# Modulation vectors of the feed-forward stages by products on VectorE

## The reference, cut to what matters

```
mod_l = split(silu(c)     @ w_mod[i] + b_mod[i], 6)      # w_mod[i]: 1024 x 6144
mod_c = split(silu(c_ctx) @ w_mod[i] + b_mod[i], 6)
x = x + mod_l[5] * (square(relu(h @ w1)) @ w2)           # w1: 1024 x 4096, w2: 4096 x 1024
```

## Time and profile before

| | us |
|---|---|
| median of 3 runs (lowest, highest) | 3954.27 (3950.56, 3956.72) |
| profiled execution, its own time | 3956.91 |
| profiled execution, span of its instructions | 3955.1 |
| TensorE busy | 3725.2 (94% of the span) |
| VectorE busy | 1968.0 (50%) |
| ScalarE busy | 1353.3 (34%) |
| GpSimd busy | 808.4 (20%) |
| `modulation_rows` in the feed-forward stages, TensorE busy | 66.3 |

### The profile page before, as it was taken

One profiled execution on the slowest core, in us unless ns is written; L12 is line 12 of the kernel. 1 busy time (PEld: TensorE's weight loads), 2 busy tenths in 40 slices (PEclk: granted clock), 3 DMA queues, 4 the chain that ended last, 5 costly groups with the idle time before them and its releaser, 6 DMA issues. The chain is left out here.

```text
span 3955.1 us, 54396 instructions
## 1 busy us (share of the span) xinstructions
PE 3725.2 (94%) x20587; PEld 2998.3 (76%) x20587; DVE 1968.0 (50%) x2905; ACT 1353.3 (34%) x2357; POOL 808.4 (20%) x604
## 2 busy tenths in 40 slices
PE   6998899999999899999999999999999988889998
PEld 4875688888878677777776688888878865577886
DVE  5746643333353474444446653333356637746445
ACT  3346532122243454232335522121224324433222
POOL 1500012212122111222220012212110018701222
PEclk9999999999999999999999999999999998999999
DMA  5234223223211311444310023323211230032222
GB/s 179 64 117 129 65 77 121 101 89 123 95 65 64 86 44 58 175 151 149 115 60 1 1 77 129 107 85 127 95 64 54 74 132 14 19 101 92 95 95 74
DMA packets 191737, 352.38 MB, mean 89 GB/s; under 512 B 41980, under 2 KB 43597, under 8 KB 191565
## 3 DMA queue, kind: packets, MB, share of 16 engines
q1 hardware_dynamic: 183789, 333.48, 25.6%
q10 hardware_dynamic: 7792, 16.78, 1.1%
HBM read 341.71 MB, written 16.92 MB: 91 GB/s over the span
## 5 line engine op out<-in xcount | busy, mean ns | idle before, releaser
L568 POOL TENSOR_TENSOR x<-x,scaled_buf 128x512 f32<-128x512 f32 (+1 forms) x360 | 465.8, 1299 | 2274.7 <-DVE scaled_buf L560 2274.1
L129 DVE TENSOR_TENSOR w_lo<-raw,w_hi 128x2048 fp32r<-128x2048 f32 x198 | 459.1, 2319 | 796.9 <-ACT w_hi L123 785.9
L123 ACT ACTIVATE w_hi<-raw 128x2048 fp32r<-128x2048 f32 x197 | 377.2, 1915 | 1190.5 <-PE psum L385 1188.0
L383 PE MATMUL psum<-hT_hi,w_hi 128*128 128x512 f32 (+1 forms) x1888 | 668.7, 354 | 2.8 <-DVE hT_lo L787 1.5
L384 PE MATMUL psum<-hT_lo,w_hi 128*128 128x512 f32 (+1 forms) x1888 | 664.9, 352 | 0.0
L385 PE MATMUL psum<-hT_hi,w_lo 128*128 128x512 f32 (+1 forms) x1888 | 664.6, 352 | 0.0
L383 PE MATMUL psum<-w_hi,uT_hi 128*128 128x512 f32 x1280 | 503.3, 393 | 0.0
L385 PE MATMUL psum<-w_hi,uT_lo 128*128 128x512 f32 x1280 | 498.6, 390 | 0.0
L384 PE MATMUL psum<-w_lo,uT_hi 128*128 128x512 f32 x1280 | 498.2, 389 | 0.0
L560 DVE TENSOR_TENSOR scaled_buf<-psum,gate 128x512 f32<-128x512 f32 x360 | 245.2, 689 | 504.3 <-PE psum L385 499.1
L383 PE MATMUL psum<-w_hi,hT_hi 128*128 128x512 f32 x1072 | 419.9, 392 | 2.2 <-issue 1.2
(11 more groups left out here) (276 smaller groups left out, 4755.2 us busy)
## 6 DMA issues: line engine op xcount, KB each, us to landing
mod_wide<-in_w_mod SPq DMA_DIRECT2D x24, 3072.0 KB, 10.5
raw<-in_w_mlp SPq DMA_DIRECT2D x64, 1024.0 KB, 5.2
raw<-in_ff_w SPq DMA_DIRECT2D x64, 1024.0 KB, 5.3
raw<-in_ssm_w_in SPq DMA_DIRECT2D x20, 1024.0 KB, 5.1
mod_slab<-in_w_mod SPq DMA_DIRECT2D x8, 2048.0 KB, 8.1
raw<-in_b_w_qkv SPq DMA_DIRECT2D x12, 1024.0 KB, 5.1
raw<-in_a_w_qkv SPq DMA_DIRECT2D x11, 1024.0 KB, 5.0
mod_first<-in_w_mod ACTq DMA_DIRECT2D x4, 2048.0 KB, 17.2
```

The source lines that it names most:

```text
L123: act.activation(K.w_hi[h][:, :, :], K.raw[h][:, :, :], ACT.Copy).then_inc(K.hi_done.h, 1)
L129: dve.tensor_tensor(K.w_lo[h][:, :, :], K.raw[h][:, :, :], K.w_hi[h][:, :, :].bitcast(F32), ALU.subtract).then_inc(K.lo_done.h, 1)
L383: pe.matmul(out, hi_a, hi_w, start=first, stop=False, **check)
L568: pool.tensor_tensor(x, x, K.scaled_buf[:, j % 2, :], ALU.add).then_inc(K.added.h, 1)
```

## The change

VectorE now makes the products. For each of the 8 blocks `k` of 128 rows and each class, it multiplies the 768 columns of `mod_wide` with one number per partition, and adds that to an accumulator in SBUF (`mod_acc`, one for each class, [128, 2, 768]): 2 operations without and 14 with a sum, 16 in all. The first 4 of a chunk stand ahead of everything else in VectorE's body, one stands after `parts` of each latent tile, and two after each of the first four gatings of `down(0, .)`. TensorE turns each accumulator with six transposes: class 0 after `down(1, 0)`, class 1 after `down(1, 2)`, both into the same two banks. VectorE sums each over the 128 partitions that now lie along a row (`modulation_sums`). TensorE's `modulation_rows` and ScalarE's copy are gone. The load comes in two halves of 1.5 MB, the first behind the loads of the up slab, the second behind those of the down slab, each once the products that read that half before are done.

```diff
     if s.count > 2:
         if stage.chunked:
             if load_mod:
-                load_mod(sp, 0)
+                for half in range(2):
+                    load_mod(sp, 0, half, again=False)
             with sp.Fori(1, s.count // 2) as c:
                 for part in range(2):
                     for h in range(2):
                         load_half(K, sp, g0 + 2 * c + part, h, s.chunk_half(c, part, h))
-                    if load_mod and part == 0:
-                        load_mod(sp, c)
+                    if load_mod:
+                        load_mod(sp, c, part)
         elif stage.unrolled:
             for n in range(2, s.count):
                 for h in range(2):
...
     mm0, re0, sq0, uh0, ul0, sc0 = (s.n for s in (K.mm_done, K.relu_done, K.sq_done, K.u_hi_done, K.u_lo_done, K.scaled))
     FB = FF_CHUNK // P
     chunks = D_FF // FF_CHUNK
-    mu0, mo0, mt0, ma0, ml0 = K.mod_used.n, K.row_out.n, K.mod_turned.n, K.mod_added.n, K.mod_loaded[0].n
+    mt0, ms0, mp0, ml0 = K.mod_turned.n, K.mod_summed.n, K.mod_product.n, [K.mod_loaded[half].n for half in range(2)]
     MOD_W = 6 * D // chunks
     if norm is not None:
         norm.added = sc0 + 2 * nt * (chunks - 1) + nt
     mod_psum = K.psum[:, 6:8, :].rearrange("p a b -> p (a b)")[:, 0:MOD_W]
-    def load_mod(sp, c):
-
-        sp.wait_ge(K.mod_used.h, mu0 + c)
-        sp.dma_start(K.mod_wide[:, :, :], mod.w[:, :, ds(c * MOD_W, MOD_W)]).then_inc(K.mod_loaded[0].h, 16)
+    def load_mod(sp, c, half, again=True):
+        if again:
+            sp.wait_ge(K.mod_product.h, 2 * KD * c + (mp0 + KD * (half - 1)))
+        k0 = half * SLAB_K
+        sp.dma_start(K.mod_wide[:, k0:k0 + SLAB_K, :], mod.w[:, k0:k0 + SLAB_K, ds(c * MOD_W, MOD_W)]).then_inc(K.mod_loaded[half].h, 16)
+    def modulation_products(dve, c, first, last):
+        for i in range(first, last):
+            k, cls = i // 2, i % 2
+            if i % KD == 0:
+                dve.wait_ge(K.mod_loaded[i // KD].h, 16 * c + (ml0[i // KD] + 16))
+            if i == 0:
+                dve.wait_ge(K.mod_turned.h, 2 * c + mt0)
+            acc, col = K.mod_acc[:, cls, :], K.cT[:, mod.layer // 2, k, cls:cls + 1]
+            if k == 0:
+                ins = dve.tensor_scalar(acc, K.mod_wide[:, k, :], col, None, ALU.mult)
+            else:
+                dve.wait_ge(K.mod_product.h, 2 * KD * c + (mp0 + i - 1))
+                ins = dve.scalar_tensor_tensor(acc, K.mod_wide[:, k, :], col, acc, ALU.mult, ALU.add)
+            ins.then_inc(K.mod_product.h, 1)
+    def modulation_sums(dve, c, cls):
+        dve.wait_ge(K.mod_turned.h, 2 * c + (mt0 + cls + 1))
+        dve.tensor_reduce(K.mod_sum[:, 0:MOD_W // P, cls:cls + 1].rearrange("p b x -> p (b x)"), mod_psum.rearrange("p (b j) -> p b j", j=P),
+                          AX.X, ALU.add).then_inc(K.mod_summed.h, 1)
     def tile_done(eng, c, which, j):
...
                     act.activation(K.relu[:, j % 2, :], K.bank[j][:, :], ACT.Relu).then_inc(K.relu_done.h, 1)
                     square(c, j)
                 split_hi(K, act, g + 1, 1)
-                if mod:
-                    act.wait_ge(K.mod_used.h, mu0 + c + 1)
-                    act.activation(K.mod_row_wide[:, :], mod_psum, ACT.Copy).then_inc(K.row_out.h, 1)
                 if ahead:
                     split_hi(K, act, g + 2, 0)
                     if not last:
...
             def body(c, ahead, last=False):
                 g = st.g0 + 2 * c
+                if mod:
+                    modulation_products(dve, c, 0, 4)
                 split_lo(K, dve, g + 1, 0)
                 for j in range(nt):
                     parts(c, j)
+                    if mod and j < FB:
+                        modulation_products(dve, c, 4 + j, 5 + j)
                 split_lo(K, dve, g + 1, 1)
                 for h in range(2):
                     for j, t in enumerate(tiles):
...
                         gate_out(K, dve, sc0 + 2 * nt * c + h * nt + j, h, t, K.bank[j], j)
                         if norm is not None and last and h == 1:
                             norm.beside(K, dve, j)
+                        if mod and h == 0 and j < FB:
+                            modulation_products(dve, c, KD + 2 * j, KD + 2 * j + 2)
+                        if mod and h == 1 and j in (0, 2):
+                            modulation_sums(dve, c, j // 2)
                     if ahead and not (last and h):
                         split_lo(K, dve, g + 2, h)
-                if mod:
-                    dve.wait_ge(K.mod_turned.h, mt0 + c + 1)
-                    mod_sums(K, dve, mod_psum, MOD_W // P).then_inc(K.mod_summed.h, 1)
-                    dve.wait_ge(K.mod_summed.h, K.mod_summed.n + c + 1)
-                    mod_add(K, dve, mod.layer, c * (MOD_W // P), MOD_W // P).then_inc(K.mod_added.h, 1)
+                    if mod and h == 1:
+                        dve.wait_ge(K.mod_summed.h, 2 * c + (ms0 + 2))
+                        mod_add(K, dve, mod.layer, c * (MOD_W // P), MOD_W // P).then_inc(K.mod_added.h, 1)
             dve.wait_ge(K.gate_done.h, K.gate_done.n)
+            if mod:
+                dve.wait_ge(K.feat_lo.h, K.feat_lo.n)
             ahead_loop(dve, st, body, hold)
         @block.gpsimd
...
                 return product(pe, K.bank[j][:, :], K.uT_hi[:, k, t * P:(t + 1) * P], K.uT_lo[:, k, t * P:(t + 1) * P],
                                K.w_hi[h][:, k, :], K.w_lo[h][:, k, :], k == 0, k == SLAB_K - 1)
-            def modulation_rows(c):
-                pe.wait_ge(K.mod_loaded[0].h, 16 * c + (ml0 + 16))
-                pe.wait_ge(K.mod_added.h, ma0 + c)
-                mod_rows(K, pe, mod_psum[:, 0:SLAB_N], mod.layer, K.mod_wide[:, :, 0:SLAB_N])
-                mod_rows(K, pe, mod_psum[:, SLAB_N:MOD_W], mod.layer, K.mod_wide[:, :, SLAB_N:MOD_W]).then_inc(K.mod_used.h, 1)
-
-            def modulation_columns(c):
-                pe.wait_ge(K.row_out.h, mo0 + c + 1)
-                mod_turns(K, pe, mod_psum, K.mod_row_wide[:, :], MOD_W // P).then_inc(K.mod_turned.h, 1)
+            def modulation_columns(c, cls):
+                pe.wait_ge(K.mod_product.h, 2 * KD * c + (mp0 + 2 * KD - 1 + cls))
+                pe.wait_ge(K.mod_summed.h, 2 * c + (ms0 + cls))
+                mod_turns(K, pe, mod_psum, K.mod_acc[:, cls, :], MOD_W // P).then_inc(K.mod_turned.h, 1)
             def chunk(c, fed):
                 g = st.g0 + 2 * c
...
                         for k in range(SLAB_K):
                             mm = down(0, j, t, k)
                     mm.then_inc((K.w_used if j == nt - 1 else K.mm_done).h, 1)
-                    if mod and j == 2:
-                        modulation_rows(c)
                 pe.wait_ge(K.lo_done.h, 2 * g + 2)
                 for j, t in enumerate(tiles):
                     pe.wait_ge(K.scaled.h, sc0 + 2 * nt * c + j + 1)
                     for k in range(SLAB_K):
                         mm = down(1, j, t, k)
                     mm.then_inc((K.w_used if j == nt - 1 else K.mm_done).h, 1)
-                    if mod and j == 2:
-                        modulation_columns(c)
+                    if mod and j in (0, 2):
+                        modulation_columns(c, j // 2)
             chunk(0, feed is not None)
             with pe.Fori(1, chunks) as c:
...
         c = Cursor(gate_at, R + R_BYTES)
         K.gate = c.put("gate", [P, 2, D])
         K.mod_wide = c.put("mod_wide", [P, KD, 6 * P])
-        K.mod_row_wide = c.put("mod_row_wide", [P, 6 * P])
+        K.mod_acc = c.put("mod_acc", [P, 2, 6 * P])
         K.lam_in = place("lam_in", [P, 4, HEAD_DIM], H + 16 * 1024)
         K.qkv = place("qkv", [P, TOK_TILES, 3 * D], R)
         c = Cursor(qkv_end, R + R_BYTES)
```

More of the change, by code:

```diff
@@ L758, in mlp_stage @@
     if mod:
-        for s in (K.mod_used, K.row_out, K.mod_turned, K.mod_summed, K.mod_added):
-            s.n += chunks
-        K.mod_loaded[0].n += 16 * chunks
+        K.mod_added.n += chunks
+        K.mod_product.n += 2 * KD * chunks
+        for s in (K.mod_turned, K.mod_summed):
+            s.n += 2 * chunks
+        for s in K.mod_loaded[0:2]:
+            s.n += 16 * chunks
 def operand_stage(K, src, k_tiles, ctx, dst_hi, dst_lo, scale=None, bias=None, norm=None, affine=None, feat=None, gate=None, gate_scale=1.0,
@@ L2922, in program @@
         K.mod_used = sem("mod_used")
+        K.mod_product = sem("mod_product")
         K.row_out = sem("row_out")
```

## The result

| | before | after |
|---|---|---|
| median (lowest, highest), 11 runs each | 3954.46 us (3950.56, 3959.33) | 3963.06 us (3958.88, 3965.67) |
| profiled execution: own time, span | 3956.91, 3955.1 | 3962.2, 3960.3 |

The ratio is 1.0021, 95% interval 1.0013 to 1.0029: slower by 8.6 us, by 5 to 11 with the interval. The forecast was 3966, slower by 12.

A forecast was written before the change was run, and what follows sets the result against it. TensorE, busy for every microsecond of the feed-forward stages, was taken as the bound; -26 (six-tile chunks), +18 (four-tile chunks), +4 (first four-tile chunk) and +16 (clock) make +12, so 3966 us on the median, range 3930 to 3993.

The forecast's parts named there:

- The lock: VectorE operations with two SBUF inputs and GpSimd's adds wait for each other whole; a tile costs VectorE 3.54 us.
- Rival C: Products do not wait for adds, so the pace is TensorE's 2.72 us a tile; 3918 us, chance 0.13.
- The order at each gating: After each gating of down(0, .) the first product starts at g + 0.61, ahead of GpSimd's add at g + 0.76.
- rival D: The add comes first at each gating; four-tile stall 6.3 us, six-tile chunks stall 1.05; 3993 us, chance 0.12.
- Six-tile chunk: Six-tile stages: second turn stalls about 0.2 us, a chunk gains 1.95; with the exceptions, sum -26 us.
- Four-tile chunk: Four-tile stage: first turn waits 4.4 us for product 15, a chunk loses 2.25; 8 chunks +18 us.
- The first four-tile chunk: Opening of the four-tile stage: half a load arrives late, products and split start late; +4.2 us once, bounds 0 and 8.
- The clock: After each four-tile stall TensorE runs at 1.2 GHz for a while; 2 us each, bounds 0 and 2.25, +16 us.
- Rival B: The clock holds through the four-tile stage's stalls; -4 us, 3950 us, chance 0.15.
- Where nothing waits: TensorE's modulation work falls from 3.65 to 1.5 us, so a chunk gains 2.15 us.
- last chunks: Ends of the six-tile stages, where VectorE ends last, normalising: first stage gain 0.8 us, third stage loss 1.05.

The follow-up runs named there:

- experiment 1: Changed kernel, but in the four-tile stage products 9 to 16 of a chunk multiply with idle PSUM banks, one SBUF input each; 3919.34 us, one run.
- experiment 2: Changed kernel, but in the four-tile stage GpSimd adds only the first 32 of 512 columns of each tile; 3919.69 us, one run.
- experiment 4: Changed kernel, but with the change in the two six-tile stages alone, rows on TensorE as before in the four-tile stage; 3928.5 us, ratio 0.9935.
- experiment 3: Changed kernel, but in the four-tile stage TensorE does 18 unused matmuls where it would wait for product 15; 3947.04 us, ratio 0.9982.
- experiment 5: Changed kernel, but with the change in the four-tile stage alone, both six-tile stages as in the kernel before; 3990.43 us, one run.
- experiment 6: Changed kernel, but in the four-tile stage accumulators turned after down(1, 2) and down(1, 3), sums moved to match, products unmoved; 3924.15 us, ratio 0.993.

## Why the prediction was right, point by point

- *The lock.* Forecast: pace 3.54, adds near 2.0, first product 1.01 and the second near 2.05. Measured 3.50, 1.99, and 2.98 for the two, so that with 0.93 for the first the second took 2.05. The mechanism was right, and not only the time. The sum was built on a case with other operations; here experiments 1 and 2 show both sides of it. The Trainium skill (SBUF — State Buffer, "Who interferes with whom") calls it an exclusive lock for the whole instruction: the 0.25 us add that takes 0.95 agrees. Rival C, that products and adds pass each other, named 3918; the kernel of experiment 1 took 3919.3, but that the two are so near is chance. There they pass in the four-tile stage alone, with a quicker operation, and this stage is 7.8 us shorter than before, where C has 4.5; and C's -32 for the six-tile stages does not follow from the terms shown (-26, and 13 times 0.2 more, are -28.6).
- *The order at each gating.* The product comes first, as taken: it starts at 1629.65, the add at 1629.81. All gatings looked at had this order; rival D did not occur. (By its own terms its stall would be 6.5 us, not 6.3: 1641.9 + 3 × 3.83 + 2.9 - 1649.8.)
- *Six-tile chunk.* Forecast 67.6, measured 67.57 in the first stage and 67.48 in the third. The second turn's 0.2 us of waiting, which no row shows as idle, can be seen from the turns' spacing, 6.32 us in the change and 6.13 where the products are spread. Sum forecast -26, measured -26.0 by the medians of experiment 4 and -28.7 by the traces of the kernels before and after.
- *Four-tile chunk.* Forecast stall 4.4, chunk 51.4; measured 4.2 and 51.3. The 7 chunks after the first lose 28.8 us (second turns from 1598.09 to 1956.87), 4.1 each, forecast 4.25.
- *The first four-tile chunk.* The extra was put at 4.2 and came out at about 3.6: the way from the stage's opening to that chunk's second turn grew by 8.0 us, 4.4 of them as in every later chunk whose turn takes 1.54 us. VectorE waits there 5.73 us for half a load, as thought; its products start at 1561.94.
- *The clock.* 2 us a chunk, taken between bounds of 0 and 2.25 from idle times at the edges of stages, measured 2.0 in the mean by experiment 3. That it was 2 and not 1 was chosen, not worked out, and came out well partly by luck. Rival B, that the clock holds through such a stall in dense work, gave 3950; it is the kernel with the stall filled that took 3947. The Trainium skill (TensorE: Matmul & The Clock Gate, "HAM oscillation — how this bites in real kernels") has such a loop, whose clock falls at each recurring wait; the trace agrees, with a granted clock of 0.95 over the stage.
- *What was mis-sized.* The forecast stood 3 us above the median. Each stage was 1.3 to 1.4 us better than its forecast, 4 us in all. In the six-tile stages more than half of it is their last chunks with what follows: the first stage gained 1.7 there, forecast 0.8; the third lost 0.3, forecast 1.05, although TensorE's idle at its end grew by 2.45 (8.38 to 10.83 in the row below). The rest is that a chunk gains 2.0 to 2.1 there, not 1.95, and loses 4.1 in the four-tile stage, not 4.25. Where nothing waits, a chunk gains 2.25 (69.58 to 67.33, 47.13 to 44.89), not 2.15.

```profile
2920.24 5.35 PE L247 MATMUL psum<-ident,x 128*128 128x128 f32 x24 [10.83 <-DVE x L299]
```

## What to carry to other kernels

Work moved to an engine with idle time is priced by what stands beside it and by who waits for its last piece: here VectorE was three quarters busy in the stage, and TensorE still stood 4 us a chunk. Two operations with two SBUF inputs in a row beside a GpSimd add cost 1 us more a pair here, one cost 0.4 or nothing, and 1.1 for the split behind the last; put an operation with a PSUM input between them, or place them where GpSimd rests. A recurring stall of TensorE is to be counted with its clock, here half as much again; the cure was to spread the same 16 products otherwise, which turned +9 us into -45.

## What the runs showed of the hardware that was not expected

- Most of a GpSimd operation's length in a trace can be waiting: 0.25 us alone, 0.95 behind a product, for 32 columns. The wait is not in the idle time before it, so the lock shows only in its length against that of the same operation alone.
- After stalls of equal length (4.20 or 4.21 us) the clock does not fall at the same place: the turn takes 1.54 in one chunk and 0.87 in the next, and the chunks are 51.5 and 50.9 us long in turn. Windows of the changed kernel behind the stall that ends at 1641.24, and behind the one that ends at 1692.76:

```profile
1641.00:1643.00 2.00, 1.76 (x7) 1.67 (x8) 2.00 (x3) 0.00 (x0) 1.23 (x1) 0.50 0.00 0
1645.00:1647.00 2.00, 2.00 (x8) 1.55 (x8) 1.72 (x3) 0.00 (x0) 1.07 (x1) 0.76 0.26 25
...
1691.00:1693.00 2.00, 0.24 (x2) 0.25 (x3) 2.00 (x4) 0.00 (x0) 1.22 (x1) 1.00 0.00 0
1695.00:1697.00 2.00, 2.00 (x6) 1.58 (x5) 2.00 (x2) 0.00 (x0) 0.00 (x0) 0.50 0.00 0
```

The first time the granted clock is at 0.50 when the work begins again, the second time it is still 1.00 and falls behind it. Against the 49.33 of the filled kernel that is 2.2 and 1.6 us. In experiment 5 the same stalls show 1.37, 1.12 and 0.87 as well. What decides where the low stretch falls was not tried.
- Stalls of 0.94 us in each chunk (experiment 6) and of 1.12 (experiment 2) left the granted clock at 1.00.
